# Seven half-width products in place of eight for the branch gates of a two-block transformer kernel

## What is computed

```python
def mixer_layer(x, mem, ...):
    h = rmsnorm(x, g_norm)
    z = jnp.einsum('bsd,dn->bsn', h, w_in)
    dq, dk, dv, dg, lq, lk, lv, lg, mq, mg, mgate = jnp.split(z, splits, axis=-1)
    ...   # three attentions: differential, dilated (3 groups), memory
    y_a = jnp.einsum('bse,ed->bsd', o_a * jax.nn.silu(dg), w_br_diff)
    y_b = jnp.einsum('bse,ed->bsd', o_b * jax.nn.silu(lg), w_br_dil)
    y_m = jnp.einsum('bse,ed->bsd', o_m * jax.nn.silu(mg), w_br_mem)
    gates = jax.nn.sigmoid(mgate).reshape(B, S, N_BRANCH, D_MODEL)
    merged = gates[:, :, 0] * y_a + gates[:, :, 1] * y_b + gates[:, :, 2] * y_m
    return x + jnp.einsum('bsd,de->bse', merged, w_out)
```

## Time and profile before

| | |
|---|---|
| median of 3 runs | 2998.32 us (2998.10 to 2998.94) |
| profiled execution | 2998.21 us, its span from first to last instruction 2996.40 us |
| TensorE matmuls / weight loads | 97% / 83% of the span, 17134 of each |
| VectorE, ScalarE, GpSimd | 54%, 42%, 6% |
| TensorE clock granted | 0.989 of full speed |
| HBM | 82 GB/s over the span |
| branch stage, blocks 1 to 3 of layer 1 | 56 us each |

### The profile page before, as it was taken

One profiled execution on the slowest core, in us unless ns is written; L12 is line 12 of the kernel. 1 busy time (PEld: TensorE's weight loads), 2 busy tenths in 40 slices (PEclk: granted clock), 3 DMA queues, 4 the chain that ended last, 5 costly groups with the idle time before them and its releaser, 6 DMA issues.

```text
span 2996.4 us, 42406 instructions
## 1 busy us (share of the span) xinstructions
PE 2900.5 (97%) x17134; PEld 2484.3 (83%) x17134; DVE 1630.7 (54%) x3223; ACT 1256.1 (42%) x2630; POOL 185.8 (6%) x207
## 2 busy tenths in 40 slices
PE   8899999999999999999999999999999999999998
PEld 7888888988887787888888888877898888888886
DVE  6776646367664454676333564335676433564334
ACT  5455423255553243565234333234565324433222
POOL 2100000020000000100000000000100000000000
PEclk9999999999999999999999999999999999999999
DMA  3111221211113222322232222233322232222222
GB/s 117 50 49 58 101 69 64 93 59 52 54 57 108 69 99 92 115 75 72 85 119 85 78 78 85 88 109 99 109 72 80 85 113 90 80 71 92 92 92 84
DMA packets 99726, 250.07 MB, mean 83 GB/s; under 512 B 8597, under 2 KB 44845, under 8 KB 99274
## 3 DMA queue, kind: packets, MB, share of 16 engines
q1 hardware_dynamic: 99530, 247.35, 25.3%
HBM read 239.60 MB, written 6.50 MB: 82 GB/s over the span
## 4 chain that ended last, share of the span: by engine, by line
PE 81%; DVE 10%; ACT 5%; issue 2%; DMA 1%; POOL 1%; SPq 0%; DVEq 0%; POOLq 0%; ACTq 0%
PE ps L93 78%; PE ps L96 3%; ACT Z L99 2%; DVE Z L102 2%; DVE Z L110 2%; DVE cl L102 1%; DMA st<-in_stream_dram 1%; ACT ch L99 1%; DVE ZR L102 1%; DVE Z L106 1%; DVE stat L123 1%; POOL stat L102 1%; DVE stat L110 1%; DVE Z L120 1%; DVE hn L110 0%
## 5 line engine op out<-in xcount | busy, mean ns | idle before, releaser
L93 PE MATMUL ps<-hl,ch 128*128 128x512 f32 (+1 forms) x2512 | 831.0, 359 | 0.0
L93 PE MATMUL ps<-hh,ch 128*128 128x512 f32 (+1 forms) x2368 | 801.6, 365 | 24.1 <-DVE cl L102 9.7
L102 DVE TENSOR_TENSOR cl<-st,ch 128x1024 fp32r<-128x1024 f32 (+1 forms) x436 | 499.9, 1154 | 568.3 <-ACT ch L99 567.1
L93 PE MATMUL ps<-hh,cl 128*128 128x512 f32 (+1 forms) x2368 | 792.2, 361 | 0.0
L99 ACT ACTIVATE ch<-st 128x1024 fp32r<-128x1024 f32 (+1 forms) x436 | 428.7, 990 | 345.6 <-PE ps L93 309.6
L93 PEld LDWEIGHTS ps<-hh,ch 128*128 128x128 f32 x2368 | 422.6, 190 | 106.4 <-ACT Z L99 14.3
L93 PEld LDWEIGHTS ps<-hl,ch 128*128 128x128 f32 x2512 | 448.1, 190 | 72.8
L93 PEld LDWEIGHTS ps<-hh,cl 128*128 128x128 f32 x2368 | 423.1, 190 | 70.7
L99 ACT ACTIVATE Z<-ps 128x512 f32<-128x512 f32 (+7 forms) x506 | 216.1, 436 | 550.8 <-PE ps L93 444.3
L93 PE MATMUL ps<-ZR,ch 128*128 128x512 f32 (+2 forms) x1680 | 437.6, 350 | 2.0 <-DVE cl L102 1.6
L93 PEld LDWEIGHTS ps<-ZR,ch 128*128 128x128 f32 x1680 | 284.5, 189 | 47.6 <-issue 3.9
(11 more groups left out here) (134 smaller groups left out, 3171.7 us busy)
## 6 DMA issues: line engine op xcount, KB each, us to landing
st<-in_stream_dram SPq DMA_DIRECT2D x372, 512.0 KB, 3.4
st<-in_stream_dram SPq DMA_DIRECT2D x64, 256.0 KB, 3.3
Z<-decay_rows SPq DMA_DIRECT2D x8, 904.0 KB, 5.4
Z<-bias_lines SPq DMA_DIRECT2D x16, 448.0 KB, 3.6
ya_spill<-Z SPq DMA_DIRECT2D x8, 512.0 KB, 4.0
Z<-ya_spill SPq DMA_DIRECT2D x2, 2048.0 KB, 7.7
Z<-in_x_dram SPq DMA_DIRECT2D x4, 512.0 KB, 5.3
Z<-in_mem_dram SPq DMA_DIRECT2D x2, 1024.0 KB, 7.0
```

The lines of the kernel that those rows point to most:

```text
L93: return Ins(self, self.e and self.e.matmul(o, a, b, start=start, stop=stop, skip_group_check=True))
L102: return Ins(self, self.e and self.e.tensor_tensor(o, a, b, op))
```

## The change

**Products.** For the 24 gate units the two projections are replaced by seven products of half-size matrices (Strassen's scheme in Winograd's form). The unit is cut in quarters of 512 features x 128 columns (A11, A12, A21, A22), the tokens' matrix h in quarters of 512 features x 256 tokens. A product is 4 k-tiles of three matmuls of 128 weight columns by 256 tokens. Product j uses

with S1 = A21 + A22, S2 = S1 - A11, S3 = A11 - A21, S4 = A12 - S2, all made on VectorE from the fp32 pieces, S3 and S4 in place. The products collect in banks 0, 1, 0, 1, 2, 1, 2; between them values are read from PSUM and combined:

```diff
+            def fp(l, bi, c, u, j):
+                key, b = ("fs", l, bi, c), (0, 1, 0, 1, 2, 1, 2)[j]
+                opens = j in (0, 1, 4)
+                if opens:
+                    pe.wait_ge(*held[b])
+                    held[b] = [("free", key, b)]
+                elif j == 2:
+                    pe.wait_ge(("p1", *key))
+                elif j == 3:
+                    pe.wait_ge(("u2", *key))
+                elif j == 5:
+                    pe.wait_ge(("u3", *key))
+                else:
+                    pe.wait_ge(("c22", *key))
...
+                for k in range(4):
+                    pe.matmul(o, wh[:, k, :], xh[:, k, :], opens and k == 0, False)
+                    pe.matmul(o, wh[:, k, :], xl[:, k, :], False, False)
+                    m = pe.matmul(o, wl[:, k, :], xh[:, k, :], False, k == 3)
+                m.then_inc("pe_fast", ("full", key, j), ("wfree", u, j))
```

**Order.** Gates of a unit and the conversions are put so, and the converted buffers are handed out in halves (512 columns, six in all):

```diff
+        def gates(bi, c, beside=lambda j: None):
+            u = self.unit(2, l, 10240 + 1024 * bi + 256 * c)[0]
+            tgs[bi, 2 * c], tgs[bi, 2 * c + 1] = tg = self.ntg(), self.ntg()
+            n = self.nsq()
+            for j in range(7):
+                put("fp", l, bi, c, u, j)
+                if j:
+                    put("fe", l, bi, c, j - 1, n, *tg)
+                    self.halves(1)
+                beside(j)
+            put("fe", l, bi, c, 6, n, *tg)
+            self.halves(2)
...
+        def first(j):
+            if j == 3:
+                put("fB", l, 2)
+            elif j in (1, 2):
+                put("tph", l, j + 1)
+                put("tpl", l, j + 1)
+        self.halves(2)
+        gates(0, 0, first)
```

```diff
+            def cv(u, j):
+                a11, a21, a12, a22 = quarters(u)
+                if j == 0:
+                    dve.wait_ge(("st", u), ("st", u + 1), *bars(("eend", stream_plan()[u][1])),
+                                *([("cl", older[u], 4)] if older[u] is not None else []))
+                    dve.tensor_tensor(S1T, a21, a22, ALU.add).then_inc("dve_wsum", ("S", u, 4))
+                    dve.wait_ge(dve.newest)
+                    dve.tensor_tensor(S2T, S1T, a11, ALU.subtract).then_inc("dve_wsum", ("S", u, 1))
+                elif j == 1:
+                    dve.tensor_tensor(a21, a11, a21, ALU.subtract).then_inc("dve_wsum", ("S", u, 3))
+                hi, lo = product(u, j)
+                dve.wait_ge(("ch", u, j), *([("S", u, j)] if j in (1, 3, 4, 6) else []))
+                dve.tensor_tensor(lo, source(u, j), hi.bitcast(F32), ALU.subtract).then_inc("dve_wlo", ("cl", u, j))
+                if j == 2:
+                    dve.wait_ge(("S", u, 1))
+                    dve.tensor_tensor(a12, a12, S2T, ALU.subtract).then_inc("dve_wsum", ("S", u, 6))
```

**Buffers.** A third staging buffer in Z serves the gate and branch pieces (`stage_ring`, `stg.append(z(24576, 1024))`), gate buffers TG are 4 in place of 6, mg's results have four of their own (GM), and branch products take single banks in turn:

```diff
-                acquire(key, "PA")
+                acquire(key, "BR")
```

More of the change, by code:

```diff
@@ L290, in half_piece, with fast_piece, conversions, halves_of @@
     return blk == 2 and what == "in" and x < 2048
+PRODUCTS = ("A11", "S2", "A12", "S3", "S1", "A22", "S4")
+N_STAGE, N_HALVES = 3, 6
+def fast_piece(r):
+    blk, _, what, x, _ = stream_plan()[r]
+    return blk == 2 and what == "in" and x >= 10240
+def conversions():
+    o, plan = [], stream_plan()
+    for r in range(len(plan)):
+        if not fast_piece(r):
+            o.append(("w", r))
+        elif plan[r][4] == 0:
+            o.extend([("cv", r, j) for j in range(7)])
+    return o
+def halves_of(task):
+    return 1 if task[0] == "cv" and task[2] < 6 else 2
+def weight_ring():
+    at, owner, before = {}, [], {}
+    for t in conversions():
+        at[t[1:]] = len(owner)
+        real = 1 if t[0] == "cv" else 2
+        waits = []
+        for h in range(len(owner), len(owner) + real):
+            g = h - N_HALVES
+            while g >= 0 and owner[g] is None:
+                g -= N_HALVES
+            if g >= 0 and ("wfree", *owner[g]) not in waits:
+                waits.append(("wfree", *owner[g]))
+        before[t[1:]] = waits
+        owner += [t[1:]] * real + [None] * (halves_of(t) - real)
+    return at, before
+def stage_ring():
+    plan, buf, prev, latest = stream_plan(), [], [], {0: -2, 1: -1, 2: -3}
+    for r, (blk, l, what, x, h) in enumerate(plan):
+        wide = fast_piece(r) or what in ("bd", "bm")
+        b = min((0, 1, 2) if wide else (0, 1), key=lambda i: latest[i])
+        buf.append(b)
+        prev.append(latest[b] if latest[b] >= 0 else None)
+        latest[b] = r
+    return buf, prev
 class Order:
@@ L666, in block2 @@
                         put("lqev", l, g, x, 2 * c + h)
+                        y = 4 * x + 2 * c + h
+                        if g == 1:
+                            put("tpn", l, y)
+                        elif g == 2 and y < 4:
+                            put("tpc", l, y)
+                        elif g == 2 and y < 6:
+                            put("tph", l, 5 - y)
+                            put("tpl", l, 5 - y)
                         if g and x and c + h == 1:
@@ L793, in block2 @@
                     put("ybs", l, k)
-            gate(2, 2 * c)
-            gate(2, 2 * c + 1)
+            gates(2, c)
             if c == 0:
@@ L1993, in scalar_program @@
                       lqev=lqev, lvev=lvev, lvp=lvp, lS=lS, lse0=lse0, mqev=mqev, lse1=lse1, lgev=lgev, eT=eT,
-                      eP=eP, yasp=yasp, fA=fA, fB=fB, mgev=mgev, gtev=gtev, ybs=ybs, yms=yms, mgs=mgs, turn=turn,
+                      eP=eP, yasp=yasp, fA=fA, fB=fB, mgev=mgev, cv=cv, tph=tph, fe=fe, ybs=ybs, yms=yms, mgs=mgs, turn=turn,
                       osq=osq, bar=act.bar)
@@ L2756, in consts @@
             def consts():
-                for r in range(NST):
-                    piece(r)
+                pieces(done)
                 sp.dma_start(ifs, I["w_if"]).then_inc("d_consts", by=16)
```

241 lines of the change are left out of this document (183 added, 58 removed).

## The result

The changed kernel takes 3007.9 us, the median of 8 runs (3003.35 to 3014.1), beside 2998.51 us for the kernel before (8 runs, 2998.01 to 2999.44). The ratio is 1.0033, its 95% interval 1.0022 to 1.0044: 0.3% slower, by little, but the interval lies outside 0.2%. The forecast was 3001.5 us, its range 2982 to 3018.

What follows compares the result with a forecast made beforehand. TensorE, busy 97% of the span, was taken as the bound. Gain of 31.4 us against waits of 11.6, 10.4, 7.0, 2.0, 3.1 and 0.5 gave +3.2 us: 3001.5 us, range 2982 to 3018.

Steps and rivals of the forecast that it cites:

- TensorE's stream: Gate units: 84 matmuls of 256 columns take 9.89 us instead of 11.20; 24 units gain 31.4 us.
- (a): Unit 1 to unit 2 of a block: P1's copy late on ScalarE, 0.92 us, 3.0 in block 0; both layers 11.6.
- (b): First unit of a layer, behind fA(3): waits of 2.3, 1.4, 0.7 and 0.8 us; both layers 10.4.
- (c): Block 0: the yms remainders queue late for branch 2's first matmul, 3.5 us a layer, both layers 7.0.
- (d): Block 3: mgs remainders ahead of branch 1's first eviction leave a bank late, about 1.0 us a layer, both 2.0.
- (e): Units followed by a branch product: a whole piece's conversion delays c22, 0.22 us at 14 places, 3.1 us.
- The sum of the branch stage: Branch stage of each layer: half the 31.4 us matmul gain set against the forecast waits there.
- The queues do not keep up: Denies the rival that queues keep up: ScalarE reaches P1 in time unless foreign work stands ahead; 2983.5 us, chance 0.27.
- the clock: TensorE's clock in the branch stage: the forecast added no time for clock falls behind its six waits above 2 us.
- the rival: Clock falls behind each of six waits above 2 us, 2.2 us each, 13 us on top: 3014.7 us, chance 0.13.
- VectorE in full: Rival: each VectorE operation starts only when the one before ends, 0.72 us not 0.61: 3016.4 us, chance 0.13.

Runs made afterwards that it cites:

- e12_c22_outer_all: Changed kernel with queues reordered and splits spread, plus c22 ahead of whole-piece conversions in units of branches 0 and 2 only: 0.9928 of the kernel before, 2975.11 us.
- e1: Changed kernel with P1's copy put ahead of two conversions on ScalarE's queue in the second unit of each pair: 1.0011 of the kernel before, 3000.15 us.
- e3: Changed kernel with fA(3) ahead of the last merge product, and token-sum conversions and fB(2) later in the first unit: 1.0030 of the kernel before, 3005.76 us.
- e0_as_changed: The changed kernel run a second time with no edit: 1.0032 of the kernel before, 3008.47 us.
- e2: Changed kernel with block 0's ybs and yms copies and remainders moved among earlier products and the units: 0.9988 of the kernel before, 2992.48 us.

## Why the prediction was right in part

- **TensorE's stream.** A matmul of 256 columns takes 0.118 us, as the rows of before said; the 84 of a unit without waits take 9.93 us (1879.84 to 1889.77 in e12_c22_outer_all), forecast 9.89. A block without waits takes 52.33 instead of 56.07 us, 3.74 of the expected 3.93.
- **(a), the pairs.** Forecast 0.92 us with the restart, and 3.0 in block 0. The weight loads' rows say 0.92 (three a layer) and 3.00, with the mechanism given: 11.5 of 11.6 us. e1 shows the cause by taking it away.
- **(b), the first unit.** The sum of 5.2 us a layer is met by luck (3.29, 0.19, 0.40 and 0.62 and their restarts, 5.3): its terms were 2.3, 1.4, 0.7 and 0.8, and the largest was the wrong wait, not P1's copy but bank 0, which fA(3) holds until its exponentials are through. I had followed the queues and not who holds the bank. e3, built on the wrong mechanism, gained 0.9 us where 4.2 to 5.6 were expected.
- **(c) and (d).** Forecast 3.5 and 1.0 a layer, measured 3.14 and 0.54 and the restarts (3.3 and 0.7).
- **(e), c22.** Forecast 0.22 us at 14 places; it is there at 14 places, 0.24 by TensorE's starts (1929.66 to 1929.92 is 0.26, the next 0.22, where 0.118 is usual).
- **The sum of the branch stage** was to be -15.7 + 17.1 = +1.4 us a layer. Layer 0, where the clock did not fall, has +1.56; that it is so close is in part luck, as (b) shows. The queues do not keep up: the waits of 0.71 and those for c22 stand in the rows, which refutes that rival.
- **The step that failed** is the clock, where the forecast took none of the six waits above 2 us to bring it down, and the rival all six at 2.2 us. Three did in the first profile. From one wait to the next (2712.28 to 2724.90, 2758.66 to 2773.68, 2773.68 to 2819.78), beside the same distances in layer 0, they cost 12.62-10.50 = 2.12, 15.02-13.50 = 1.52 and 46.10-43.47 = 2.63 us, 6.3 in all. 3010.11 less 6.3 is 3003.8, and the fastest run took 3003.35. The rival had the right mechanism and, for these three, the right price (2.1 us on the mean), and its count was an outcome that varies between executions: half of it on top, 3001.5 + 6.6 = 3008 us, would have met the median, but that is said with the result known. The spread of the runs, 3003 to 3014 where the kernel before has 2998.0 to 2999.4, fits zero to five falls. The mean granted clock of each run goes with it: the runs of 3003.35 and 3005.19 us have 0.987, that of 3014.1 has 0.985, the other five 0.986; of the second series (e0_as_changed) the run of 3001.05 us, the profiled one with a single fall, has 0.989, that of 3002.58 has 0.988, and the four of 3007.24 to 3010.46 have 0.986 or 0.985. So a slower run had the lower clock for longer. Where in such a run it fell, and whether that is the whole of the spread, these means do not show.
- **VectorE in full** is refuted. Its operations on 512 columns start 0.60 to 0.61 us apart in the changed kernel too (1856.56, 1857.16, 1857.76), as in the earlier trace rows. The Trainium skill's rule in "VectorE: DVE Perf Modes", "The DRAIN you can't avoid", by which the next operation does not start before the pipe is empty, is not what these rows show; the section says itself that an operation that is not held starts earlier.
- The 1.16 us at layer 1's start, with the fall behind it, was in no term.

What stays open: why, of two equal waits, one brings the clock down. None of the rows compared here tells the two apart before the fall.

## What to carry to other kernels

A change that takes work from the bound engine is worth what the queues of the others let through: here the 31 us of matmuls went into waits at places where something less urgent stood ahead of the operation wanted next, and into falls of the clock behind them, and moving it brought the kernel from 0.3% above the one before to 0.7% below it. Write the queues out by hand with distances from the trace, which gave the waits between the units to a tenth, and write beside each wait who holds the bank, which would have found the largest one. Spread what is not urgent one by one, move an operation only where something is gained, and put on top of a long pause of TensorE the price of a fall of the clock, here 1.1 to 2.6 us, times how often one came: in four of 16 pauses of 1.6 to 2.3 us, in 26 of 42 of 2.6 us and more.

## What the runs showed of the hardware

Over the changed kernel and the twelve experiments' traces, the branch stages have 58 waits of TensorE of 1.6 us or more. Behind 30 the granted clock went to 0.50: 26 of the 42 of 2.6 us and more, 4 of the 16 of 1.6 to 2.3. Behind the shorter ones of these stages, 1.58 and less (14 of them over 1 us), never. One fall costs 1.07 us (the first unit in e1 and e2: 11.57 instead of 10.50), 1.20, 1.52, 2.12 or 2.63, with the matmuls of 256 columns 0.21 us apart while it lasts. The dear ones last longer: in the changed kernel the clock is at 0.50 from 2759.1 to 2762.4 us in the fall of 1.52 us, and from 2711.3 to 2718.0 in that of 2.12. The same wait at the same place falls in one execution and not in the next, in two units of one execution too. At layer 1's start the three waits of 2.29 to 2.75 us had a fall behind them, the eleven of 1.37 and less none. In every trace, that of before among them, the pauses at some 1706 and 2610 us, 2.4 and 1.5 to 2.0 us with tiny matmuls between, were followed by a fall.
